# Head-norm weights as per-partition scales of ScalarE's copies of the turned rows, in place of wide VectorE multiplications

## The reference, cut to what matters

```python
def _rmsnorm(t, w):
    tf = t.astype(jnp.float32)
    y = tf * lax.rsqrt(jnp.mean(tf * tf, axis=-1, keepdims=True) + RMS_EPS)
    return (y * w.astype(jnp.float32)).astype(t.dtype)
...
dq = _rmsnorm(da_q.reshape(B, S, DA_HEADS, 2, DA_HEAD_DIM), da_q_norm_w[l])
dk = _rmsnorm(da_k.reshape(B, S, DA_HEADS, 2, DA_HEAD_DIM), da_k_norm_w[l])
...
o_da = _rmsnorm(o_da, da_out_norm_w[l]) * (1.0 - lam_init)
...
o_gla = _rmsnorm(o_gla, gla_out_norm_w[l]).reshape(B, S, GLA_HEADS * GLA_DV) * jax.nn.silu(gl_r)
...
xq = _rmsnorm(xa_q.reshape(B, S, XA_HEADS, XA_HEAD_DIM), xa_q_norm_w[l])
mk = _rmsnorm(mk.reshape(B, M, XA_HEADS, XA_HEAD_DIM), xa_k_norm_w[l])
```

## Time and profile before

| | |
|---|---|
| median of 3 runs | 3668.76 us (3667.63 to 3668.84) |
| the profiled execution's own time | 3662.57 us |
| its span | 3660.8 us |
| instructions | 31,972 |
| PE / DVE / ACT / POOL busy | 2839.5 / 2241.9 / 688.1 / 1165.4 us |
| mean granted TensorE clock | 0.879 of full speed |
| DMA moved | 1304.38 MB, of it 1078.00 MB by GpSimd's queue |
| first gather starts | 516.22 us |

### The profile page before, as it was taken

The page is one execution under the profiler, slowest core; times in us unless marked ns, Lnnn a source line. Parts: engine busy times, 40 slices in busy tenths (PEclk is TensorE's granted clock), DMA queues, the critical chain, the costliest instruction groups (busy, mean ns, idle before and its releaser), DMA issues. The chain is left out here.

```text
span 3660.8 us, 31972 instructions
## 1 busy us (share of the span) xinstructions
PE 2839.5 (78%) x11208; PEld 1442.3 (39%) x11208; DVE 2241.9 (61%) x5637; ACT 688.1 (19%) x1255; POOL 1165.4 (32%) x1036
## 2 busy tenths in 40 slices
PE   8889867799987867799988767889987835555555
PEld 3567723346635313355635313345653501111111
DVE  1231287875545887775545887775454787666665
ACT  2320112621111113521111113531111100000000
POOL 0000023443322333443323333443332334444442
PEclk9999988899998978999999878899998967777777
DMA  5324559999999999999999999999999969999998
GB/s 174 101 98 152 176 207 398 398 419 418 413 419 358 398 371 368 388 393 411 413 418 393 387 364 369 367 376 406 413 418 398 410 229 400 421 420 415 421 421 334
DMA packets 212737, 1304.38 MB, mean 356 GB/s; under 512 B 25424, under 2 KB 26464, under 8 KB 80992
## 3 DMA queue, kind: packets, MB, share of 16 engines
q0 software_dynamic: 148608, 1078.00, 72.6%
q1 hardware_dynamic: 63968, 224.33, 16.7%
HBM read 1288.61 MB, written 13.63 MB: 356 GB/s over the span
## 5 line engine op out<-in xcount | busy, mean ns | idle before, releaser
L634 POOL DMA_INDIRECT rowbuf<-in_peer_uv,idx x884 | 1001.1, 1132 | 2209.0 <-PE acc L931 1531.6
L931 PE MATMUL acc<-rowbuf,diag 128*64 128x512 f32 x3536 | 1065.6, 698 | 427.4 <-DVE diag L1617 420.0
L1607 DVE CUSTOM_DVE_ANT_0 rowbuf<-rowbuf,xr 128x1024 f32<-128x1024 f32 x884 | 1059.8, 1222 | 319.3 <-DMA rowbuf<-in_peer_uv,idx 319.2
L931 PEld LDWEIGHTS acc<-rowbuf,diag 128*64 128x64 f32 x3536 | 260.1, 153 | 1039.7 <-DVE diag L1617 550.3
L1198 ACT ACTIVATE acts<-dots 128x2 f32<-128x2 f32 x512 | 104.1, 203 | 2295.4 <-DVE dots L1607 2247.4
L1617 DVE TENSOR_SCALAR diag<-consts,acts,gw 128x64 f32<-128x64 f32 x1024 | 286.7, 350 | 270.7 <-ACT acts L1198 124.8
L683 PE MATMUL bank<-xnT,W 128*128 128x256 f32 x1600 | 366.2, 385 | 0.0
L669 PE MATMUL bank<-W,xnT 128*128 128x512 f32 x736 | 334.6, 605 | 0.5 <-ACT kv L984 0.5
L683 PEld LDWEIGHTS bank<-xnT,W 128*128 128x128 f32 x1600 | 300.5, 191 | 86.0 <-issue 47.9
L683 PE MATMUL bank<-arena,W 128*128 128x256 f32 x1024 | 245.6, 399 | 55.4 <-DMA W<-in_w_blocks 54.3
L931 PE MATMUL acc<-kv,diag 128*64 128x512 f32 x440 | 206.6, 802 | 86.6 <-DVE diag L1617 86.6
(11 more groups left out here) (193 smaller groups left out, 2344.3 us busy)
## 6 DMA issues: line engine op xcount, KB each, us to landing
W<-in_w_blocks SPq DMA_DIRECT2D x360, 512.0 KB, 7.9
rowbuf<-in_peer_uv,idx POOLq DMA_INDIRECT x884, 15.4
xs<-in_x SPq DMA_DIRECT2D x16, 512.0 KB, 8.2
xr<-x SPq DMA_DIRECT2D x32, 256.0 KB, 12.6
out_y<-xs SPq DMA_DIRECT2D x8, 512.0 KB, 7.7
x<-arena SPq DMA_DIRECT2D x8, 512.0 KB, 22.7
out_y<-xr POOLq DMA_DIRECT2D x8, 512.0 KB, 17.1
xs<-memory SPq DMA_DIRECT2D x3, 1024.0 KB, 9.0
```

The lines of the kernel that those rows point to most:

```text
L634: pool.indirect_dma_start(rows[SLOT[g]], None, a["peer_uv"], bass.IndirectOffsetOnAxis(ap=idx[:, at // NB, at % NB:at % NB + 1], axis=0)). ...
L931: mm = pe.matmul(acc[HP * j:HP * (j + 1), h * HALF:(h + 1) * HALF], diag[:, c % DIAGS, j, :], v[:, D + h * HALF:D + (h + 1) * HALF], start ...
L1607: dve.tensor_tensor_reduce(out=u, in0=u, in1=xr[:, t, j, :], scale=1.0, scalar=0.0, op0=ALU.mult, op1=ALU.add, accum_out=dots[:, c % QS, j ...
```

## The change

The weights are left out where the norm is applied, and go in where ACT copies the turned rows out of the bank: there a weight belongs to a partition, and the copy takes it as its scale operand. The six vectors come as one table `w_norm` of 128x6, arranged on the host (the two 64-long ones repeated twice). The 8 score factors of Q are multiplied into the reciprocals (128x16) instead. `merge` no longer multiplies the weights into the gate. DA's constant 0.2 is multiplied into one column. K, Q, XQ and MK's transposes wait for the bank's release by L1265. The tiles `w_q64`, `w_qs`, `w_k64`, `w_dao`, `w_glo`, `w_xq` and `w_xk` (4,608 bytes of each partition) make way for `w_norm` (24 bytes), and all tiles that are allocated after them move down.

```diff
-        w_q64 = sb("w_q64", [P, DA_D])
-        w_qs = sb("w_qs", [P, 2 * DA_H, DA_D])
-        w_k64 = sb("w_k64", [P, DA_D])
-        w_dao = sb("w_dao", [P, DA_V])
-        w_glo = sb("w_glo", [P, GL_V])
-        w_xq = sb("w_xq", [P, XA_D])
-        w_xk = sb("w_xk", [P, XA_D])
+        w_norm = sb("w_norm", [P, 6])
+        w_key, w_query, w_xq, w_xk, w_dao, w_glo = (w_norm[:, i:i + 1] for i in range(6))
...
-            (w_q64[:, :], a["q_w"].partition_broadcast(P)), (w_k64[:, :], a["k_w"].partition_broadcast(P)),
-            (w_dao[:, :], a["dao_w"].partition_broadcast(P)), (w_glo[:, :], a["glo_w"].partition_broadcast(P)),
-            (w_xq[:, :], a["xq_w"].partition_broadcast(P)), (w_xk[:, :], a["xk_w"].partition_broadcast(P)),
+            (w_norm[:, :], a["w_norm"]),
...
-                         [(hn_done, norm_no("K", n))])
+                         [evacuated(("K", n))])
...
-            def copy(job, dst, *shape):
+            def copy(job, dst, *shape, weight=None):
...
-                act.activation(dst, view(job, *shape), ACT.Copy).then_inc(free_sem(job), 1)
+                scale = {} if weight is None else {"scale": weight}
+                act.activation(dst, view(job, *shape), ACT.Copy, **scale).then_inc(free_sem(job), 1)
...
-                    copy(("KT", n, t), kv[:, g + t, 0, :].rearrange("p (h s) -> p h s", h=DA_H), DA_H, P)
+                    copy(("KT", n, t), kv[:, g + t, 0, :].rearrange("p (h s) -> p h s", h=DA_H), DA_H, P, weight=w_key)
...
-                    copy(("QT", n, t), qT[:, :, t * P:(t + 1) * P], DA_H, P)
+                    copy(("QT", n, t), qT[:, :, t * P:(t + 1) * P], DA_H, P, weight=w_query)
...
-                copy(("XQT", n), xqT.rearrange("p a b -> p (a b)"), 1024)
+                copy(("XQT", n), xqT.rearrange("p a b -> p (a b)"), 1024, weight=w_xq)
...
-                copy(("OT", n, 0), oT[0].rearrange("p a b -> p (a b)"), 1024)
+                copy(("OT", n, 0), oT[0].rearrange("p a b -> p (a b)"), 1024, weight=w_dao)
...
-                copy(("OT", n, 1), oT[1].rearrange("p a b -> p (a b)"), 1024)
+                copy(("OT", n, 1), oT[1].rearrange("p a b -> p (a b)"), 1024, weight=w_glo)
...
-            def norm_heads(no, src, dst, groups, width, weight, release=None, squares=sq):
+            def norm_heads(no, src, dst, groups, width, weight=None, release=None, squares=sq, factor=None):
...
                 after(dve.reciprocal(hs[:, 2, 0:groups], hs[:, 1, 0:groups]))
+                if factor is not None:
+                    rs = hs[:, 2, 0:groups].rearrange("p (t g) -> p t g", t=NT)
+                    after(dve.tensor_tensor(rs, rs, factor, ALU.mult))
                 ins = dve.tensor_tensor(dst, src, wide(hs[:, 2, 0:groups].unsqueeze(2), groups, width), ALU.mult)
                 if release is not None:
                     ins.then_inc(free_sem(release), 1)
-                    dve.wait_ge(*evacuated(release))
+                elif weight is None:
+                    ins.then_inc(hn_done, 1)
                 else:
                     after(ins)
-                dve.tensor_tensor(weight[0](dst), weight[0](dst), weight[1], ALU.mult).then_inc(hn_done, 1)
+                    dve.tensor_tensor(dst, dst, weight, ALU.mult).then_inc(hn_done, 1)
...
-                g3 = gr.rearrange("p t (h d) -> p (t h) d", d=GL_V)
-                dve.tensor_tensor(g3, g3, wide(w_glo[:, :].unsqueeze(1), 8, GL_V), ALU.mult).then_inc(gr_ready, 1)
-                dve.wait_ge(gr_ready, n)
...
-            dve.tensor_tensor(w_qs[:, :, :], wide(w_q64[:, :].unsqueeze(1), 2 * DA_H, DA_D), wide(qscale.unsqueeze(2), 2 * DA_H, DA_D), ALU.mult)
-            dve.tensor_scalar(w_dao[:, :], w_dao[:, :], 1.0 - LAM_INIT, None, ALU.mult)
+            dve.tensor_scalar(w_dao, w_dao, 1.0 - LAM_INIT, None, ALU.mult)
```

More of the change, by code:

```diff
@@ L765, in memory_attention @@
                     pe.wait_ge(memory_in, 16 * (n - 1))
-                turn(("XQT", n), [xq[:, t, h, :] for h in range(XA_H) for t in range(NT)], [(hn_done, norm_no("XQ", n))])
+                turn(("XQT", n), [xq[:, t, h, :] for h in range(XA_H) for t in range(NT)], [evacuated(("XQ", n))])
                 for t in range(NT):
@@ L874, in merge @@
                     token_major(("GR", n), xnT)
-                turn(("OT", n, 0), [oda[:, t, h, :] for h in range(4) for t in range(NT)], [(hn_done, norm_no("DA", n))])
+                turn(("OT", n, 0), [oda[:, t, h, :] for h in range(4) for t in range(NT)], [(hn_done, 2 * n - 1)])
                 some(n, 4)
-                turn(("OT", n, 1), [ogl[:, t, h, :] for h in range(4) for t in range(NT)], [(hn_done, norm_no("GLA", n))])
+                turn(("OT", n, 1), [ogl[:, t, h, :] for h in range(4) for t in range(NT)], [(hn_done, 2 * n)])
                 for hf in range(2):
@@ L953, in _ @@
                     token_major(("MV", 0), memT)
-                    turn(("MKT", 0), [xq[:, t, h, :] for h in range(XA_H) for t in range(NT)], [(hn_done, 1)])
+                    turn(("MKT", 0), [xq[:, t, h, :] for h in range(XA_H) for t in range(NT)], [evacuated(("MK", 0))])
                     project_front(1)
@@ L1215, in _ @@
                     copy(("MV", 0), memory(0)[2].rearrange("p a b -> p (a b)"), 1024)
-                    copy(("MKT", 0), memory(0)[1].rearrange("p a b -> p (a b)"), 1024)
+                    copy(("MKT", 0), memory(0)[1].rearrange("p a b -> p (a b)"), 1024, weight=w_xk)
                     project_front(1)
@@ L1290, in keys @@
             def keys(n):
-                norm_heads(norm_no("K", n), view(("K", n), 16, DA_D), heads_of(kn), 16, DA_D,
-                           (grouped, wide(w_k64[:, :].unsqueeze(1), 16, DA_D)), ("K", n), sq_front)
+                norm_heads(norm_no("K", n), view(("K", n), 16, DA_D), heads_of(kn), 16, DA_D, release=("K", n), squares=sq_front)
             def queries(n):
@@ L1296, in queries @@
                 dve.wait_ge(*filled(("KT", n, 1)))
-                norm_heads(norm_no("Q", n), view(("Q", n), 16, DA_D), heads_of(qn), 16, DA_D,
-                           (by_tile, wide(w_qs[:, :, :].unsqueeze(1), NT, 2 * DA_H, DA_D)), ("Q", n), sq_front)
+                norm_heads(norm_no("Q", n), view(("Q", n), 16, DA_D), heads_of(qn), 16, DA_D, release=("Q", n), squares=sq_front,
+                           factor=wide(qscale.unsqueeze(1), NT, 2 * DA_H))
             def project(n):
                 if n == 1:
-                    norm_heads(norm_no("XQ", n), view(("XQ", n), 8, XA_D), heads_of(xq), 8, XA_D,
-                               (grouped, wide(w_xq[:, :].unsqueeze(1), 8, XA_D)), ("XQ", n))
+                    norm_heads(norm_no("XQ", n), view(("XQ", n), 8, XA_D), heads_of(xq), 8, XA_D, release=("XQ", n))
                 picks.upto(("GL", n))
@@ L1408, in gla @@
                 picks.upto(("GV", n))
-                norm_heads(norm_no("DA", n), heads_of(oda[:, :, :, :]), heads_of(oda[:, :, :, :]), 8, DA_V,
-                           (grouped, wide(w_dao[:, :].unsqueeze(1), 8, DA_V)))
+                norm_heads(norm_no("DA", n), heads_of(oda[:, :, :, :]), heads_of(oda[:, :, :, :]), 8, DA_V)
                 dve.wait_ge(gla_ops, n)
@@ L1444, in merge @@
                     dve.wait_ge(*evacuated(job))
[L1445 to L1447 removed]
                 norm_heads(norm_no("GLA", n), heads_of(ogl[:, :, :, :]), heads_of(ogl[:, :, :, :]), 8, GL_V,
[L1449 removed]
+                           weight=gr.rearrange("p t (h d) -> p (t h) d", d=GL_V))
                 for hf in range(2):
@@ L1663, in _ @@
                     take_x(1)
-                    norm_heads(1, view(("MK", 0), 8, XA_D), heads_of(xq), 8, XA_D, (grouped, wide(w_xk[:, :].unsqueeze(1), 8, XA_D)), ("MK", 0))
+                    norm_heads(1, view(("MK", 0), 8, XA_D), heads_of(xq), 8, XA_D, release=("MK", 0))
                     keys(1)
@@ L1691 @@
         "w_gg": np.ascontiguousarray(np.asarray(w_in)[0][:, C_GG:C_GG + GL_R]),
-        "q_w": np.asarray(da_q_norm_w)[0], "k_w": np.asarray(da_k_norm_w)[0], "lam": np.asarray(da_lambda).reshape(-1),
-        "dao_w": np.asarray(da_out_norm_w)[0], "w_gate": np.asarray(gla_w_gate)[0], "b_gate": cols(gla_b_gate),
-        "glo_w": np.asarray(gla_out_norm_w)[0], "xq_w": np.asarray(xa_q_norm_w)[0],
-        "xk_w": np.asarray(xa_k_norm_w)[0], "ffn_w": np.asarray(ffn_norm_w)[0],
+        "lam": np.asarray(da_lambda).reshape(-1), "w_gate": np.asarray(gla_w_gate)[0], "b_gate": cols(gla_b_gate),
+        "w_norm": np.stack([np.tile(np.asarray(da_k_norm_w)[0], 2), np.tile(np.asarray(da_q_norm_w)[0], 2), np.asarray(xa_q_norm_w)[0],
+                            np.asarray(xa_k_norm_w)[0], np.asarray(da_out_norm_w)[0], np.asarray(gla_out_norm_w)[0]], axis=1),
+        "ffn_w": np.asarray(ffn_norm_w)[0],
         "w_blocks": weight_blocks({
```

8 lines of the change are left out of this document (1 added, 7 removed).

## The result

The changed kernel takes 3627.41 us (3624.68 to 3634.84, 4 runs) beside 3668.2 us (3667.13 to 3668.84, 4 runs) for the kernel before: a ratio of 0.9898, 95% interval 0.9886 to 0.9910, 40.8 us less. Forecast were 3657.4 us and a range of 3640 to 3669, so the gain is more than three times the forecast's 11.4 us and outside its range.

The account below looks back on a forecast made before the run. It took mixer work to bound the kernel up to the first gather, then the DMA, with DVE the bound in dry stretches. Steps 1 to 4 gave 2.2 + 1.15 + 3.8 + 4.25 = 11.4 us: 3657.4 us, range 3640 to 3669.

Parts of the forecast that it names:

- rival 4: Tiles move; `rowbuf` starts on a multiple of 256, runs touch 32 lines, not 33: 33 us less, 3624; chance 0.07.
- Idle DMA time: (1.01 - share) x 20 per 20 us stretch after the first gather; saved DVE work counts only where gathers wait for buffers.
- MK, K(1), Q(1), XQ(1), DA(1): Weight multiplications of the memory's keys and step 1's K, Q, XQ, DA: hidden behind other PE work, 0 us.
- GLA(1): Gate's weight multiplication in step 1, ahead of GLA's norm: on the path, so PE, SP and the step come 1.25 us earlier.
- XQ(2): XQ's weights in step 2: PE waits 3.22 us before the turned queries, DMA later idles 2.6 us; 1.25 us won.
- First gather at 514.0: Sign of the forecast: step 1's net saving of 2.2 us brings the first gather from 516.22 to 514.0 us.
- GLA(2), DA(2): Weight multiplications between 770 and 830 us in step 2: 0 us, as the DMA doesn't run dry again in that step.
- DA(3), GLA(3): Weight multiplications in step 3: only 1.0 us of idle DMA time at 1660 left to win; 0.8 us taken.
- K and Q of steps 2 to 4: Weight multiplications there: K 1.25 us and Q 0 in step 2; K 1.25 and Q 1.0 in steps 3 and 4 each.
- Rival 1: Gathers take the saving back; only 2.2 us before the first gather counts: 3666.6 us, no change; chance 0.28.
- Rival 2: Every saved DVE instruction counts, as slots, mixers and copies form one chain: 25 us less, 3643.8; chance 0.07.
- Rival 3: At the steps' ends more gathers precede SP's store of x2, 5.4 us more at three gates: 3675.1, slower; chance 0.08.

Follow-up runs that it names:

- p1: Kernel before with only `rowbuf` moved, to 128 bytes past a multiple of 256: 3658.59 us, ratio 0.9993 to before.
- p2: Kernel before with only `rowbuf` moved, to 32 bytes past a multiple of 256: 3661.99 us, ratio 1.0000 to before.
- e8: The kernel before, unchanged, run and profiled again: ratio 0.9999 to before.
- e2: Changed kernel with an unused 4,576-byte tile, so that all later tiles keep their old addresses: 3649.15 us, ratio 0.9941 to before.
- q0: e2 repeated, as the level for kernels with added work: 3650.16 us, ratio 0.9967 to before.
- r2: e2 for the third time, beside r1: 3648.73 us, ratio 0.9966 to before.
- e1: Kernel before plus one unused 32-byte tile, giving `kv`, `W`, `rowbuf` the changed kernel's places within 256 bytes: 3651.48 us, ratio 0.9951.
- e3: Kernel before with only `rowbuf` moved, onto a multiple of 256 bytes: 3647.73 us, ratio 0.9929 to before.
- e4: Kernel before with gaps putting `kv`, `W`, `xs`, `xr` and `rowbuf` all on multiples of 256 bytes: 3645.64 us, ratio 0.9940.
- r1: The changed kernel, unchanged, measured on another occasion: 3623.10 us, ratio 0.9894 to before.
- q2: q0 plus 18 idle DVE multiplications, 6 ahead of each GLA norm of steps 2 to 4: 3661.02 us, ratio 0.9999 to before.
- p4: e2 plus 21 idle DVE multiplications: 3 before each DA norm, 6 before GLA's and 3 before Q's in step 2: 3652.07 us, ratio 0.9978.
- q1: q0 plus 18 idle DVE multiplications, 6 ahead of each DA norm of steps 2 to 4: 3672.74 us, ratio 1.0024 to before.
- e5: e2 with 8 DVE multiplications, by ones, put back for K and Q: 3657.41 us, ratio 0.9967 to before.
- e7: e2 with 20 DVE multiplications, by ones, put back for K, Q, XQ, DA and GLA's gate: 3671.47 us, ratio 1.0001 to before.
- p5: q0 plus 18 idle DVE multiplications, one before each wait for PE's BR bank in steps 2 to 4's merges: 3649.57 us, ratio 0.9963.

## Why the prediction was wrong, and what of it held

**The step that failed** is rival 4's case against itself: "`kv`, `W` and `rowbuf` differ in their offsets today, and the last stretches run at 421 GB/s through all of them". From this the tiles' places were booked at 0 and given a chance of 0.07. The row is right, the inference is not: 128 and 224 are both off a multiple of 256, and p1 and p2 show that `rowbuf` costs alike at 32, 128 and 224. A comparison in which nothing starts on a multiple can't speak about starting on one. The places are worth 18.5 to 25.6 us, about half of the result in the first comparison and nearly two thirds in the last.

Rival 4's own time, 3624, was near (3627.41) by luck, since its errors offset each other. It took 3.0% a gather, and the rates show 1.4%; it took the DMA as full for half of the time; and it put the saved work at 11.4 us. With 1.4%, 884 gathers x 2.49 us x 0.014 = 30.8 us if every one counted; measured are 18.5 to 25.6, so six to eight tenths of it arrive.

**The forecast's sum** of 11.4 us was near two of the three measurements and too low for the other. Its counterpart, the saved work at the old places, came out at 20.9, 12.1 and 14.2 us. This kernel stayed within 1.5 us in the three measurements (3649.15, 3650.16, 3648.73), while the kernel before lay at 3670.0, 3662.2 and 3662.9. So this spread comes with the kernel before (the changed kernel moved by 4.3 us between its two measurements); why it is some 8 us slower on some occasions is open. There is a lead in its two profiles, of 3662.57 us and, in e8, 3669.24: from 2460 to 2480 us the granted clock is 0.83 in the first and 0.66 in e8, e8's DMA share then is 0.94 and 0.95 up to 2540 where the first has 1.01 to 1.02 until 2520, and its last store of x2 starts 7.3 us later. No run tests it.

**Idle DMA time** was the quantity that the sum went by. Taken as in the prediction, (1.01 - share) x 20 over all 20 us stretches from 520 to 3600 us, it is 109.8 and 114.6 us in the two profiles of the kernel before, and 104.4, 99.6 and 104.8 in those of the saved work alone (e2, q0, r2): some 9 us less. By steps, the forecast expected 1 us less in step 2 and 3 to 4 in each of steps 3 and 4. Found are 7.1 against 5.9 on average up to 1140 us, so nothing gained, then 3.5 us less up to 1960 and 6.1 less up to 2840. The faster gathers leave the DMA idle for longer, 130.6, 128.0 and 121.0 us in e1, e3 and e4, some 14 more than before, which fits that only part of the 30.8 us arrives. The changed kernel has 115.8 and 104.8 (r1).

Item by item:

- *MK, K(1), Q(1), XQ(1), DA(1): 0.* No run contradicts it, none tests it alone.
- *GLA(1): 1.25 us.* Held. The timeline of the changed kernel has the three instructions and no weights' between them, and PE's wait for W, 7.30 us in the earlier trace rows, is 7.12:

```profile
253.48 1.22 DVE L1429 TENSOR_TENSOR arena<-rowbuf,arena 128x1024 f32<-128x1024 f32 x1 [2.53 <-ACT arena L1140]
254.74 1.22 DVE L1256 TENSOR_REDUCE hs<-arena 128x8 f32<-128x1024 f32 x1
...
257.82 1.22 DVE L1269 TENSOR_TENSOR xs<-xs,arena 128x1024 f32<-128x1024 f32 x1
...
267.38 8.86 PE L883 MATMUL bank<-arena,W 128*128 128x256 f32 x27 [7.12 <-DMA W<-in_w_blocks]
```

- *XQ(2): 1.25 of PE's 3.22 us.* The wait did shrink, to 1.95 us. That the DMA's idle time behind it shrank with it is not shown (step 2 above).

```profile
605.69 1.06 PE L686 MATMUL bank<-consts,arena 128*128 128x128 f32 x8 [1.95 <-DVE arena L1262]
```

- *First gather at 514.0.* It is at 517.62 in the changed kernel's profile, 515.6 in r1 and 514.9 in r2, against 516.22 before. From the start of step 1's gate projection (115.61 before, 118.6 after) to the first gather it is 400.6 and 399.1 us, 1.5 us less where the forecast has 2.2; the late start is not the change's, since e1 and e3, with the old work, have it too (118.3, 118.6).
- *GLA(2), DA(2): 0, because the DMA doesn't run dry again.* Doubtful for GLA(2): PE's stop shrinks by 1.26 us, and q2, with doses at GLA in steps 2 to 4, costs 10.9 us and has a dry stretch at 840 (share 0.75) where q0 has 1.01 to 1.02 all around. *DA(3), GLA(3): 0.8*: the stops shrink by 0.51 + 1.26. If PE's stops were prices, 1.26 for GLA(2), 0.53 for DA(2) and 0.51 + 1.26 - 0.8 in step 3 would come on top: 11.4 + 2.8 = 14.2 us, within the three measurements; after p4 this is an argument and not shown. The mistake in the reasoning was to ask only whether the DMA was full in that stretch. The ring of row buffers carries a delay on: q1 has its added work in step 2 from 769 to 777 us and runs dry from 800 on, q2 has it from 828 to 836 and runs dry from 840 on.
- *K and Q of steps 2 to 4: 1.25 + 2 x 2.25 = 5.75 us.* e5 measured 8.3 for K and Q with step 1's; the difference is within the intervals.
- *Copies: 0.1 us each.* Held: 0.087. *Q's factor 0.25 us*: 0.174.
- *The last 600 us stay as long as they are.* Wrong, by the step that failed: from the last store of x2 on, r1 takes 8.9 us less than r2.
- Two slips change nothing: the DMA's first tenths in the earlier trace rows go down to 2, not 3, and the chances of "within 0.2%" add up to 0.37.

**Rival 1** (the gathers take it back) is out: it has 2.2 us for the saved work, which alone gave 12.1 to 20.9. **Rival 2** (every saved instruction counts, 25 us) fits e7's 22.3 us and not the 12.1 and 14.2 of the other occasions. As a mechanism for any place p5 refutes it, since 18 instructions in the merges cost nothing, and p4 too; for the places of the saved instructions themselves it is not refuted on the first occasion. **Rival 3** (the gate at the steps' ends) did not come: x2's landing is 22.2 us in the median, and PE's stops for W at the ends of steps 2 to 4, of the changed kernel, sum to 45.6 us (40.7 in r1) against 43.2 in the earlier trace rows, with one of the three longer, 15.53 in place of 10.29:

```profile
1130.13 8.66 PE L675 MATMUL bank<-arena,W 128*128 128x256 f32 x32 [18.22 <-DMA W<-in_w_blocks]
...
1947.11 9.76 PE L675 MATMUL bank<-arena,W 128*128 128x256 f32 x32 [15.53 <-DMA W<-in_w_blocks]
...
2811.99 5.65 PE L675 MATMUL bank<-arena,W 128*128 128x256 f32 x16 [11.83 <-DMA W<-in_w_blocks]
```

## What to carry to other kernels

When an edit removes or adds tiles, work out where the large DMA targets come to lie, and when all of them share a property today, such as none starting on a multiple of 256 bytes, treat its effect as unmeasured: a kernel with one unused 32-byte tile settles it. Whether an instruction may count is asked of who stands behind it (here PE, stopped behind the norm for the slots' diagonals), and not only of whether another resource looks full in that stretch. How much it counts, neither tells: stops that grew by 12 us cost 2 to 4. A dose of added work must be as small as what it stands for: six instructions in one place cost their full length, three nearly nothing.

## What the runs showed of the hardware

- In a stretch full of gathers of 8 KB runs, of which 132 of 202 go to `rowbuf`, the DMA moves 426 GB/s when `rowbuf` starts on a multiple of 256 bytes of the partition, and 420 to 421 when it starts 32, 128 or 224 bytes past one, at the same DMA share of 1.01. To move the targets of the other 70 from 128 bytes past a multiple onto one changed nothing (212.84 and 212.96 MB in 500 us).
- A per-partition scale on a ScalarE copy of 1,024 columns out of PSUM costs 87 ns (1014 to 1101 ns).
- A stop of TensorE of 5.49 us was followed by a granted clock of 0.51 over the next stretch and by adds that take 3.68 us in place of 1.94; after stops of 4.27 and 4.28 us they took 3.68 too, after one of 1.72 us 1.94. A long stop is not the only thing that goes before a fall: in e8 the adds at 781.29 us take 3.92 us, 6 us after a stop of only 0.53.
- One and the same kernel had medians of 3661.2 to 3670.9 us on different occasions, twice on the same chip (3670.0 and 3661.2), more than the intervals within one occasion; the changed kernel had 3627.4 and 3623.1.
